# Sample attention in two rounds at a time, store waits carried over stage ends, and a reordered output stage, first expert block and last stage in a hybrid decoder layer

## What is computed

```python
s_c = einsum('qhgd,nhd->qhgn', q, kc) * scale            # 63 compressed keys
p_c = masked_softmax(s_c, m_c, -1);  o_c = p_c @ vc
imp = einsum('qhgn,nj->qhj', p_c, cmp_to_sel(...))        # importance of 64-row blocks
_, idx = lax.top_k(where(forced, FORCE_SCORE, imp), 8)    # selected blocks
p_s = masked_softmax(q @ k_sel * scale, ...);  o_s = p_s @ v_sel
p_w = masked_softmax(q @ win_k * scale, ...);  o_w = p_w @ win_v
out = g0 * o_c + g1 * o_s + g2 * o_w
```

## Time and profile before

| | us |
|---|---|
| median of 3 runs (lowest, highest) | 2091.45 (2086.78, 2093.21) |
| the profiled execution | 2081.51 |
| its span | 2079.8 |
| PE, DVE, ACT, POOL busy | 1783.8, 1466.6, 1099.2, 296.3 |
| granted TensorE clock, mean | 0.913 |

### The profile page before, as it was taken

The page is one execution under the profiler, slowest core; times in us unless marked ns, Lnnn a source line. Parts: engine busy times, 40 slices in busy tenths (PEclk is TensorE's granted clock), DMA queues, the critical chain, the costliest instruction groups (busy, mean ns, idle before and its releaser), DMA issues. The chain is left out here.

```text
span 2079.8 us, 27155 instructions
## 1 busy us (share of the span) xinstructions
PE 1783.8 (86%) x8975; PEld 1382.4 (66%) x8975; DVE 1466.6 (71%) x1413; ACT 1099.2 (53%) x1034; POOL 296.3 (14%) x327
## 2 busy tenths in 40 slices
PE   4999576787756398589999999999999999999981
PEld 3777464655534344478888888888888888888870
DVE  4421266355432245589999999999999999999983
ACT  3211333344321113167777777777777777777761
POOL 0000101110011140102121121212121212112110
PEclk9999877968978688599999999999999999999996
DMA  9253433230022440479999999999999999999963
GB/s 360 97 197 122 78 131 104 80 102 1 1 62 62 164 125 21 179 311 361 371 370 369 366 375 368 364 383 359 377 368 371 375 370 372 374 369 370 370 231 108
DMA packets 112151, 516.61 MB, mean 248 GB/s; under 512 B 25869, under 2 KB 47261, under 8 KB 59450
## 3 DMA queue, kind: packets, MB, share of 16 engines
q1 hardware_dynamic: 98666, 485.71, 62.5%
q0 software_dynamic: 13424, 30.12, 5.4%
HBM read 502.75 MB, written 31.81 MB: 257 GB/s over the span
## 5 line engine op out<-in xcount | busy, mean ns | idle before, releaser
L2221 PE MATMUL banks<-split 128*128 128x512 f32 x4608 | 1078.3, 393 | 1.6 <-DVE split L2365 1.6
L2221 PEld LDWEIGHTS banks<-split 128*128 128x128 f32 x4608 | 861.3, 189 | 194.2 <-issue 14.7
L2365 DVE TENSOR_TENSOR split<-expert_buffers,split 128x2048 fp32r<-128x2048 f32 x384 | 867.3, 2286 | 63.8 <-ACT split L2299 62.7
L2299 ACT ACTIVATE split<-expert_buffers 128x2048 fp32r<-128x2048 f32 x384 | 732.1, 1916 | 260.9 <-PE banks L2221 235.4
L2158 POOL TENSOR_TENSOR expert_buffers<-expert_buffers 128x1 f32<-128x1 f32 x63 | 61.0, 969 | 907.8 <-PE banks L2228 527.8
L444 PE MATMUL banks<-w_in_high,hT_high 128*128 128x476 f32 (+1 forms) x240 | 93.0, 387 | 7.7 <-DVE hT_low L370 7.7
L444 PE MATMUL banks<-w_in_low,hT_high 128*128 128x476 f32 (+1 forms) x240 | 91.3, 380 | 0.0
L444 PE MATMUL banks<-w_in_high,hT_low 128*128 128x476 f32 (+1 forms) x240 | 91.0, 379 | 0.0
L1784 PE MATMUL banks<-arena 128*128 128x512 f32 (+1 forms) x160 | 76.2, 639 | 14.4 <-DMA arena<-in_b_router 14.4
L383 DVE COPY arena<-banks 128x476 f32<-128x476 f32 (+1 forms) x15 | 9.8, 651 | 111.3 <-PE banks L444 111.3
L2369 DVE TENSOR_TENSOR split<-banks,split 128x1024 fp32r<-128x1024 f32 x64 | 77.8, 1215 | 0.0
(11 more groups left out here) (340 smaller groups left out, 1849.8 us busy)
## 6 DMA issues: line engine op xcount, KB each, us to landing
expert_buffers<-in_w_gate SPq DMA_DIRECT2D x128, 1024.0 KB, 7.7
expert_buffers<-in_w_up SPq DMA_DIRECT2D x128, 1024.0 KB, 6.6
expert_buffers<-in_w_down SPq DMA_DIRECT2D x128, 1024.0 KB, 9.1
arena<-in_w_ada SPq DMA_DIRECT2D x16, 1024.0 KB, 4.9
w_in_landing<-in_w_in SPq DMA_DIRECT2D x6, 1904.0 KB, 15.7
arena<-in_w_ada SPq DMA_DIRECT2D x4, 2048.0 KB, 19.1
arena<-in_x_prompt SPq DMA_DIRECT2D x8, 512.0 KB, 10.6
arena<-in_cache_cmp POOLq DMA_DIRECT2D x32, 128.0 KB, 3.3
```

What stands on the lines that cost most here:

```text
L2221: last = pe.matmul(ps[:, bank + c, :], x[:, kt * P:(kt + 1) * P].bitcast(F32R), wt.bitcast(F32R), start=False, stop=(kt == KT - 1 and x is ...
L2299: act.activation(high[:, j % RING_Q].bitcast(F32R), v, ACT.Copy).then_inc(s_high, 1)
L2365: dve.tensor_tensor(rest[:, j % RING_Q].bitcast(F32R), v, high[:, j % RING_Q], ALU.subtract).then_inc(s_rest, 1)
```

## The change

1. **Stage ends.** SP no longer waits for the modulation stores at the end of `project`, but in `gla` ahead of the page numbers; the wait for the key/value stores moves from the end of `gla` to that of `compress`; the last row stores of sample attention are waited for in the output stage, which also reads them back.
2. **Sample attention.** Slots for six sequences (`HELD = 6`) are filled during prompt attention. Compressed scores, fresh-key scores, compressed softmax, importance and top-k mask are made for all four rounds at once. Transposed keys, scores and masked scores have two buffers, and PE issues `scores(i + 1)` ahead of `turn_weights(i)` and `values(i)`. In `values` the two sequences alternate, matmul by matmul. SP stores the rows, POOL no longer does.
3. **Output stage.** `w_out` comes in two halves, then the router weight and the read-back, then x and the rest; PE waits for the halves separately and not for the bias. `ranks(t - 2)` moves into `project_out(t)`; ACT copies the transposed rows ahead of the next tile's statistics; tables and ranks at the end have a new order. The overflow matmuls and their table move to the experts.
4. **Experts.** No constants are loaded, one weight part is split ahead of the rows in place of four, and `overflow()` runs after the gate product of block 1. SP issues the loads of the sums at the end of this stage, after waiting for the last added rows; POOL waits no more.
5. **Combine.** Statistics come in two groups of tiles, 0 to 2 and 3 to 4.

```diff
-                             mod[32 * j:32 * j + 9, 1:3, :]).then_inc(s_modout, 16)
-            sp.wait_ge(s_modout, 64)
+                             mod[32 * j:32 * j + 9, 1:3, :]).then_inc(core.s_modout, 16)
...
+            sp.wait_ge(core.s_modout, 64)
...
-            sp.wait_ge(core.s_kvout, core.n_kvout)
...
+            sp.wait_ge(core.s_kvout, core.n_kvout)
...
+HELD = 6
...
-            load_past(core, pool, 1)
-            load_past(core, pool, 3)
+            for b in range(1, HELD, 2):
+                load_past(core, pool, b, past_numbers(core, pool, b))
...
+            rounds += [("k", i + 2, r) for r in range(6)]
+    LATE = HELD // 2
...
+            for b in range(HELD, NSEQ, 2):
+                pages = past_numbers(core, sp, b)
+                sp.wait_ge(s_pv, (b - HELD) // 2 + 1)
+                load_past(core, sp, b, pages)
+            for i in range(NU):
+                sp.wait_ge(s_res, i + 1)
+                for s in range(2):
+                    for h in range(KVH):
+                        sp.dma_start(nsa_d[h, :, 2 * i + s, :, :],
+                                     res[64 * s + 32 * h:64 * s + 32 * h + 32, i % 2, h * HD:(h + 1) * HD]
+                                     ).then_inc(s_rout[i % 2], 16)
...
+            turn("k", 0)
+            window(0)
+            turn("k", 1)
+            exps(0)
...
-                turn(number[("p", i, r)] for r in range(4))
+                    window(i + 1)
+                turn("p", i)
+                if i + 1 < NU:
+                    exps(i + 1)
+                if i + 2 < NU:
+                    turn("k", i + 2)
...
+            def masked(i):
+
+                s, w = ss[i % 2], ws[i % 2]
+                dve.wait_ge(s_sc, i + 1)
+                if i >= 2:
+                    dve.wait_ge(s_tr, number[("p", i - 2, 3)] + 1)
+                dve.tensor_copy(s[:, PAST:NKS], fresh[:, i, 0, :])
+                link(dve.tensor_copy(w[:, SEQ:NKW], fresh[:, i, 1, :]))
+                dve.wait_ge(s_wc, i + 1)
+                link(dve.tensor_reduce(mx[:, i, 1:2], w, AX.X, ALU.max))
+                negated(mx[:, i, 1:2]).then_inc(s_mw, 1)
+                dve.tensor_tensor(s[:, 0:PAST].rearrange("p (k n) -> p k n", k=NBLK_S),
+                                  ps[:, A:A + 2, :].rearrange("p a n -> p (a n)").rearrange("p (k n) -> p k n", k=NBLK_S),
+                                  bcast(bm[:, i, :], 2, 64), ALU.add).then_inc(s_taken, 1)
+                dve.wait_ge(s_taken, i + 1)
+                link(dve.tensor_reduce(mx[:, i, 0:1], s, AX.X, ALU.max))
+                negated(mx[:, i, 0:1]).then_inc(s_ms, 1)
...
+            link(dve.tensor_reduce(mxc, ps[:, O, CMP:CMP + NU * NCMP_S].rearrange("p (i n) -> p i n", i=NU), AX.X, ALU.max))
+            negated(mxc).then_inc(s_mc, 1)
+            turn("k", 0)
+            dve.wait_ge(s_ec, 1)
+            link(dve.tensor_scalar(coc, suc, 1e-30, None, ALU.max))
+            link(dve.reciprocal(coc, coc))
+            link(dve.tensor_tensor(pc[:, :, 0:NCMP_S], pc[:, :, 0:NCMP_S], bcast(coc, 2, NCMP_S), ALU.mult))
+            link(dve.tensor_reduce(im, pc.rearrange("p i (j n) -> p i j n", n=4), AX.X, ALU.add))
+            dve.tensor_tensor(im[:, :, 1:16], im[:, :, 1:16], pc[:, :, 3:63:4], ALU.add).then_inc(s_im, 1)
+            turn("k", 1)
...
+                last = dve.max(v8[:, i, :], sc[:, i, :])
+            link(last)
...
+            dve.wait_ge(s_fc, 1)
+            masked(0)
...
+                if LATE <= i + 2 < NU:
+                    turn("k", i + 2)
...
-                    pe.wait_ge(s_ms, i)
-                    pe.wait_ge(s_mw, i)
...
+                    pe.wait_ge(s_taken, i)
+                    pe.wait_ge(s_wc, i)
...
+                def group(br, terms):
+                    for k, (w, v) in enumerate(terms):
+                        for s in range(2):
+                            c = slice(64 * s, 64 * s + 64)
+                            last = pe.matmul(ps[c, O, br * P:(br + 1) * P], w[:, c], v[s], start=(k == 0),
+                                             stop=(k == len(terms) - 1))
...
+            last.then_inc(s_fs, 1)
             keys(0)
             scores(0)
+            keys(1)
+            pe.wait_ge(s_im, 1)
+            pe.matmul(ps[:, O, IMP:IMP + NU * 16], core.const("same_q"), im.rearrange("p i n -> p (i n)"), start=True, stop=True
+                      ).then_inc(s_imp, 1)
             for i in range(NU):
-                pe.wait_ge(s_im, i + 1)
...
                 if i + 1 < NU:
-                    keys(i + 1)
                     scores(i + 1)
-                weights(i)
+                turn_weights(i)
+                if i + 2 < LATE:
+                    keys(i + 2)
+                values(i)
+                if LATE <= i + 2 < NU:
+                    keys(i + 2)
...
-            sp.dma_start(wout, io["w_out"].rearrange("a (p k) n -> (a p) k n", k=KT)).then_inc(s_wo, 16)
+            w_out = io["w_out"].rearrange("a (p k) n -> (a p) k n", k=KT)
+            for a, sem in ((0, s_wo), (KT // 2, s_half)):
+                sp.dma_start(wout[:, a:a + KT // 2, :], w_out[:, a:a + KT // 2, :]).then_inc(sem, 16)
+            sp.dma_start(wr, io["w_router"].rearrange("a (p k) n -> (a p) k n", k=KT)).then_inc(s_rt, 16)
+            for u in range(2):
+                sp.wait_ge(core.s_rout[u], 64 * NSEQ // 4)
+            sp.dma_start(mix[0:NSEQ * TS, ST, 512:1024].rearrange("p (q d) -> p q d", d=HD),
+                         core.nsa_d.rearrange("h g b t d -> (b t) (h g) d")).then_inc(s_back, 16)
...
-            sp.dma_start(wr, io["w_router"].rearrange("a (p k) n -> (a p) k n", k=KT)).then_inc(s_rt, 16)
             sp.dma_start(br, io["b_router"].to_broadcast([P, NE])).then_inc(s_rt, 16)
...
+            sp.wait_ge(s_mta, NT)
+            sp.wait_ge(s_mtd, NT)
             for i, name in enumerate(("b_gate", "b_up", "b_down")):
...
+                if t == ST:
+                    pe.wait_ge(s_back, 16)
...
-            pe.wait_ge(s_rt, 32)
...
                 for kt in range(KT):
+                    if kt == KT // 2:
+                        pe.wait_ge(s_half, 16)
+                        if t >= 2:
+                            ranks(t - 2)
...
+            def turn_rows(t):
+                n = TILES[t][1]
+                pe.wait_ge(s_h, t + 1)
+                to_feature_major(h2[0:n, t % 2, :], n, 0).then_inc(s_htp, 1)
...
-                pe.wait_ge(s_h, t + 1)
-                to_feature_major(h2[0:n, t % 2, :], n, 0).then_inc(s_htp, 1)
                 pe.wait_ge(s_ht, t + 1)
+                pe.wait_ge(s_rt, 32)
...
-                else:
-                    pe.wait_ge(s_place, t)
+                elif t < NT:
+                    pe.wait_ge(s_took, t)
...
                 project_out(t)
                 if t >= 1:
+                    turn_rows(t - 1)
                     route(t - 1)
-                if t >= 2:
-                    ranks(t - 2)
             pe.wait_ge(s_res, NT - 1)
-            for t in range(NT - 2):
-                table(t)
+            table(0)
+            table(1)
             ranks(NT - 2)
+            table(2)
+            turn_rows(NT - 1)
             route(NT - 1)
             table(NT - 2)
             ranks(NT - 1)
+            ranks(NT)
             table(NT - 1).then_inc(s_tb, 1)
-            ranks(NT)
-            pe.wait_ge(s_over, 1)
-            for t, (t0, n) in enumerate(TILES):
-                for j in range(TOPK):
-                    last = pe.matmul(ps[:, 7, 0:2 * OVER], at_row[0:n, t, j, :], at_over[0:n, t, j].rearrange("p w k -> p (w k)"),
-                                     start=(t == 0 and j == 0), stop=(t == NT - 1 and j == TOPK - 1))
-            last.then_inc(s_ob, 1)
...
+            preload()
             for t, (t0, n) in enumerate(TILES):
+                if t >= 1:
+                    rows_T(t - 1)
...
-                act.wait_ge(s_htp, t + 1)
...
+                if t >= 1:
+                    weights(t - 1)
...
                 if t >= 2:
+                    take_rank(t - 2)
                     place(t - 2)
+            take_rank(NT - 2)
             place(NT - 2)
...
-                    sp.dma_start(dst, core.io["consts"][:, at:at + n]).then_inc(s_const, 16)
...
+            sp.wait_ge(s_yo, 16 * nb)
+            for t, (t0, n) in enumerate(TILES):
+                sp.dma_start(core.f[0:n, t, :], core.ffn_d[t0:t0 + n, :]).then_inc(core.s_f[t], 16)
...
+            pool.wait_ge(s_tab, 1)
...
-            pool.wait_ge(s_yo, 16 * nb)
...
+                if is_zero(done):
+                    pe.wait_ge(s_tab, 1)
+                else:
                     pe.wait_ge(s_y, done)
...
+            def overflow():
+
+                for t, (t0, n) in enumerate(TILES):
+                    for j in range(TOPK):
+                        last = pe.matmul(ps[:, DB, 0:2 * OVER], core.at_row[0:n, t, j, :],
```

(22 more changed lines are left out.)

431 lines of the change are left out of this document (222 added, 209 removed).

## The result

| | before | changed |
|---|---|---|
| median (lowest to highest, runs) | 2089.99 (2086.78 to 2093.21, 4) | 2006.07 (2003.50 to 2009.09, 4) |
| ratio, 95% interval | | 0.9605 [0.9583, 0.9626] |
| profiled execution, its span | 2081.51, 2079.8 | 2008.63, 2006.9 |
| granted clock, mean | 0.913 | 0.921 |

The change saves 82.6 us by the ratio (78 to 87), where 77.6 were forecast; the median of 2006 lies within the range, 8 under the forecast. The two profiled executions are only 72.9 apart. The part on the stages ahead comes back to this: the one of before lies 8.5 under its kernel's median, the one of the changed kernel 2.6 over.

What follows compares the result with a forecast made beforehand. PE paces the experts' unchanged loop; gains lie in sample attention, the output stage and stage heads and tails. -1.7 - 49 - 4.5 - 16.3 - 6.4 + 5.2 - 4.9 = -77.6, median 2014, range 2001 to 2034.

Steps and rivals of the forecast that it cites:

- -49 and -4.5: Sample attention: last result 49.4 us earlier through the new order (-49), and a shorter exit, 3.2 in place of 7.7 (-4.5).
- The chain worked out: Sample attention's new order timed step by step from scores 0 to the last result at 648, in place of 697.4.
- Values were priced at 4.7: Sample attention: alternating halves make 60 records take 4.7 us in place of 7.66; bounds 3.8 and 7.66.
- The row of the prompt: Prompt attention's values in the trace: 32 records in alternating halves, 0.078 us each, taken as the price for sample attention's values.
- the rival that rests on the rule: Sample attention: values don't overlap and stay at 7.66; +12, total 2026; chance 0.1.
- forecast -16.3: Output stage: projection starts earlier (-6), last ranks come together (-3.5), overflow matmuls and table leave (-6.8).
- The middle, 92.8 us of projection, DVE and routing: Output stage between head and end: PE busy nearly throughout, so 0, at most -2.
- -6.4 and +5.2: Experts: earlier rows with one part first and no constants (-6.4); 40 overflow records at 0.13 added on PE (+5.2).
- the sums' loads leave 1.4 earlier: Combine's start: DVE's wait of 3.58 shrinks by the earlier issue of the loads, -1.4.
- DVE's queue: Rival: sample attention is bound by DVE's queue (masking ahead of copies) or by late pages; +10, 2024; chance 0.12.
- The heads were shortened: Against the rival that a late store or `g_ffn` gates DVE in the output stage; +9, 2023; chance 0.07.
- The loop's period: Rival: experts' clock falls or DVE is late every block, making the kernel slower; 2116 at clock 0.90; chance 0.03.

Runs made afterwards that it cites:

- experiment 1: Changed kernel with the alternating halves undone: in values all products of sequence 0 come first, then sequence 1's; 2019.81, ratio 0.9676.
- Experiment 9: Kernel before with one wait added: POOL splits the biases only when the next rows of tile 0 are ready; 2084.62 against 2088.55, ratio 0.9978.
- experiment 5: Changed kernel, but DVE copies round i's transposed weights out before masking round i + 1; 2003.02, ratio 0.9604.
- experiment 8: Changed kernel with four weight parts split ahead of the experts' first rows in place of one, constants still out; 2015.18, ratio 0.9650.
- experiment 6: Changed kernel with the 20 overflow matmuls ahead of block 1's gate product, not behind it; 2004.58, ratio 0.9600.
- experiment 11: Changed kernel with the last stage's statistics in one group of five tiles; 2009.25.
- experiment 10: Changed kernel, but POOL waits for the last added rows and SP loads the sums in the last stage, as before the change; 2016.36, ratio 0.9659.
- experiment 7: Changed kernel with the overflow matmuls and their table back at the end of the output stage; 2009.01, ratio 0.9624.
- experiment 3: Changed kernel with slots for four sequences in place of six; 2035.27, ratio 0.9750.
- experiment 12: Changed kernel with DVE's copies of transposed weights ahead of its masking and the overflow matmuls ahead of block 1's gate product; 1995.86, ratio 0.9547.
- experiment 4: Changed kernel with one round in flight: scores, masking and exponentials of round i + 1 go behind values of round i; 2022.53, ratio 0.9674.
- experiment 2: Kernel before with only the two sequences alternating in the values; 2073.74 against 2088.68, ratio 0.9919.

## Why the prediction was right, and where it was off

**Sample attention, forecast -49 and -4.5, measured -53.7.** The chain worked out holds nearly step by step, counted from the stage's start: scores 0 end at 15.4 us (forecast 15.2), scores 1 at 28.4 (29.2), values 0 at 42.0 (43.5), values 1 at 56.4 (57.1), values 2 at 75.8 (76.0), values 3 at 82.8 (84.2). Within it errors cancel. Values were priced at 4.7 and take 4.09 at full clock; but I priced all four alike, and two of them run at a mean clock of 0.71 and 0.56, behind the wait for DVE's copies that the chain did contain, so that the four take 20.8 us for 18.8. The last result comes 84.0 us behind the start (forecast 85.3), and the exit took 4.6 us from there, not 3.2. The order of the chain was right; that the sum is right to 0.2 us is luck.

**The rule against it.** The row of the prompt was the better guide: 7.69 us come back as soon as the halves follow one another (experiment 1), and the rival that rests on the rule is out. The sentence in the Trainium skill ("TensorE: Matmul & The Clock Gate", Part 3: Packing small matmuls), that a weight load overlaps matmuls in flight only where the row groups differ, does not describe this pair: both halves use the same rows, and 60 records take 0.068 us each in place of 0.128, while by their own records a load lasts 0.13 us and a matmul 0.27 (its end is modelled), so that each load stands beside matmuls that are not done.

**Output stage, forecast -16.3, measured -21.6.** The projection starts 15.3 us into the stage (forecast 14.7, before 20.7). From the end of the last projection to DVE's last instruction it is 33.8 us, as forecast (33.9; 37.4 before). The step that failed is "The middle, 92.8 us of projection, DVE and routing, has PE busy nearly throughout, and I leave it: 0", with at most -2. It lost 6.4. The causes were there to be read: with the projection 5.5 us earlier in the stage and the biases asked for as late as ever, tile 0's rows are through before POOL starts to split biases. Experiment 9 shows that alone to be enough: same place of the split, 86.6 us. The mechanism shows on tile 1's rows in the changed kernel, DVE first, then POOL:

```profile
715.42 6.61 DVE L2077 SCALAR_TENSOR_TENSOR arena<-arena 128x1024 f32<-128x1024 f32 x1
```

```profile
714.82 6.13 POOL L1844 TENSOR_TENSOR arena<-arena 32x3072 f32<-32x3072 f32 x1
```

DVE's instruction, 1.28 us by itself, ends at 722.03, 1.08 us behind POOL's end at 720.95. In experiment 5 the two that POOL's L1844 meets (696.00 and 703.84) also end 1.08 us behind it. So DVE is stopped until POOL is done rather than slowed. The Trainium skill ("SBUF — State Buffer", Who interferes with whom) says that a DVE instruction with two SBUF inputs contends with a GpSimd instruction that reads SBUF, that the ports they share are locked for one of them at a time, and that the order of issue decides who blocks; in these three rows POOL came first and DVE stood, as that says.

**Experts, forecast -1.2, measured -1.2**, by parts -6.4 and +5.2. Measured: the head 7.3 earlier (and by experiment 8 worth 4.8 of stage, without the constants), overflow 4.66 us plus about 1.8 in slower matmuls behind it (1.87 for 1.05, and 12.16 for 11.17), the first products 1.5 slower, and the stage's end 2.7 us nearer to POOL's last add (12.7 before, 9.9 now). Three of these stood in no forecast (+1.8, +1.5 and -2.7); that they leave -1.2 is luck. What I did overlook is that block 1 waits 4.1 us for DVE: the overflow matmuls could stand there for next to nothing (experiment 6, -6.1).

**Combine, forecast -4.9, measured -7.3.** The grouping is worth 3.2 (forecast 3.5, experiment 11). The step that was mis-sized is "the sums' loads leave 1.4 earlier". I priced the issues alone. The loads' landing also lies beside the meeting of the engines now, so DVE's wait of 3.58 goes whole, and POOL's drain of 5.2 us no longer stands behind its wait: together 6.5 us from the last add to the first sum (experiment 10), of which some show in the experts' window.

**The stages ahead, forecast 0, measured +11.6.** Most of it belongs to the execution and not to the change. Prompt attention in four profiles; the first is of before, then experiments 6, 7 and 3, in columns as in the earlier trace rows:

```profile
408.00:562.70 154.70, 119.62 (x928) 80.85 (x928) 81.54 (x239) 66.80 (x258) 10.38 (x21) 0.79 0.13 42
```

```profile
409.80:573.10 163.30, 127.39 (x928) 85.65 (x928) 81.48 (x239) 67.08 (x258) 15.43 (x29) 0.74 0.18 59
```

```profile
408.10:560.90 152.80, 114.38 (x928) 77.99 (x928) 81.34 (x239) 66.09 (x258) 15.39 (x29) 0.82 0.19 63
```

```profile
410.80:571.90 161.10, 126.22 (x928) 84.78 (x928) 81.59 (x239) 66.91 (x258) 10.39 (x21) 0.75 0.12 40
```

The same 928 records take 114 to 127 us of PE, and PE's time times its clock is 94 in all four (119.62 x 0.79 = 94.5, 127.39 x 0.74 = 94.3, 114.38 x 0.82 = 93.8, 126.22 x 0.75 = 94.7). The shortest of all, 152.8, has six slots, so loading more is not the cause. Three profiles of kernels with before's code in this stage give 154.7, 157.5 and 157.4, and nine more of the changed code 152.8 to 163.3, mostly about 160. Over GLA, compress and prompt attention together the mean is 327.4 us in the three profiles with before's code (324.1 to 329.3) and 332.0 in the ten with six slots (324.3 to 335.7). So a tilt of some 5 us against the change is not excluded, and what it would come from was not tried; the rest of the 11.6 is the place of these two profiles. That is also why 72.9 us lie between the profiles and 83.9 between the medians: of the difference, 8.5 and 2.6 are the places of the two profiled executions among their own runs. The forecast of 77.6 lies between the two, 4.7 over the profiles' difference and 6.3 under the medians'. The output stage and combine gave 7.7 us more than it had, and what the three stages ahead may have taken back is in no term of it.

**Rivals.** Values did not stay at 7.66. DVE's queue does hold PE up, 3.1 to 3.7 us in three rounds, but the chain had it. Pages were not late. The heads were shortened. The loop's period is unchanged: its clock is 0.98, DVE's load 1084.75 us (1083.95 before).

## What to carry to other kernels

Two short products that share no output partitions were worth alternating record by record: some 15 us for swapping two loops. When a wait is moved to another engine, look at what its own engine does behind it at the stage's end. After a batch of work is moved, look in each in-order queue for what now stands ahead of the instruction that another engine waits for, and look in the consumer's timeline for the existing waits into which displaced work would fit; both together gave 10 us more here. And a profile is one execution: compare a stage with its own clock, and with the same stage in kernels that don't touch it, before it counts for or against a change.

## What the runs showed of the hardware

- **The clock was lower behind waits of 3 to 4 us, and behind one stretch of narrow matmuls.** In the changed kernel the clock was 1.00 in values 0, then after waits of 3.69 us a mean of 0.71 and 0.56 in values 1 and 2; with waits of 0.83 us ahead (experiment 5) the same records take 4.09 us. Behind the overflow matmuls, in which PE was busy without a gap on 34 columns, it was 0.87; without them ahead (experiments 6 and 7), the same 48 records took 11.17 us in place of 12.16. In experiment 6 the mean was 0.89 over the overflow matmuls, with no wait ahead of them, and 0.83 over the products behind. That it is their narrowness was not tried apart. Four windows of the changed kernel:

```profile
624.20:630.00 5.80, 5.78 (x61) 4.82 (x62) 0.33 (x2) 0.06 (x1) 0.00 (x0) 0.71 0.49 169
642.40:649.40 7.00, 6.88 (x60) 5.51 (x60) 0.38 (x3) 0.11 (x2) 0.00 (x0) 0.56 0.00 0
851.90:856.60 4.70, 4.70 (x42) 4.60 (x41) 2.93 (x2) 2.97 (x2) 0.00 (x0) 1.00 1.01 424
856.60:870.00 13.40, 13.40 (x56) 11.29 (x57) 8.93 (x8) 6.78 (x4) 0.00 (x0) 0.87 0.62 220
```

- **A cliff in an untouched stage.** In ten kernels whose output stage is the changed kernel's to the instruction, POOL starts the bias split 37.9 to 40.0 us into the stage in six (experiments 1, 3, 8, 10, 11 and the changed kernel), PE does not wait for tile 1's rows, and the stage takes 138.0 to 139.4; POOL starts at 40.9 to 41.4 in three (12, 5, 6), PE waits 1.28 to 1.60 us for those rows, and the stage takes 141.3 to 141.7; at 45.8 (experiment 4) PE waits 3.04 us and the stage takes 144.2. What differs is when the biases have landed, and so on which of DVE's instructions POOL's of 6 us fall.
- **POOL's DRAIN at a stage's end.** In all fourteen profiles POOL's last indirect add has landed 5.9 to 6.3 us behind its issue, whoever waits for it. In the four in which POOL waits (the kernel before, experiments 2, 9 and 10) its drain follows the wait and takes 5.20 us each time; in the ten in which SP waits it begins before the add has landed, lasts 8.7 to 9.1 us and ends beside SP's issues. What the drain waits for no run shows.
